# The last attention tile's output product in four pieces with turned tiles between them, and the first MLP product split by token columns

## The reference, cut to what matters

```python
out_a = gqa_axial_attention(qa, ka, va)            # 8 heads of 64: columns 0:512
ob = differential_attention(qb, kb, vb, lam, rel_bias)
out_b = rmsnorm(ob, b_subln_g) * (1.0 - lambda_init)   # 4 heads of 128: columns 512:1024
mixed = jnp.concatenate([out_a, out_b], axis=-1)
x = x + jnp.einsum('bse,ed->bsd', mixed, w_out)

h = rmsnorm(x, mlp_norm_g)
u = jnp.einsum('bsd,df->bsf', h, w_up)             # 1024 -> 4096
u = jnp.square(jax.nn.relu(u))
x = x + jnp.einsum('bsf,fd->bsd', u, w_down)       # 4096 -> 1024
```

## Time and profile before

| | us |
|---|---|
| median of 3 runs | 2272.73 |
| lowest and highest of them | 2269.25, 2276.43 |
| the profiled execution, its own time | 2264.31 |
| its span | 2262.5 |

### The profile page before, as it was taken

How to read it: one execution, slowest core, us unless ns; L and a number is a source line. 1 busy time by engine, 2 the same in 40 slices (tenths; PEclk the granted TensorE clock), 3 DMA queues, 4 the chain that set the end, 5 groups by cost and what they waited for, 6 DMA issues and landing times. The chain is left out here.

```text
span 2262.5 us, 21742 instructions
## 1 busy us (share of the span) xinstructions
PE 2056.5 (91%) x6808; PEld 1127.2 (50%) x6808; DVE 1324.0 (59%) x3030; ACT 880.8 (39%) x2292; POOL 936.7 (41%) x621
## 2 busy tenths in 40 slices
PE   6999998999898989888589999999989998999999
PEld 5787543333333333333233333333345555888887
DVE  6333457777777777787465456465556653433432
ACT  2453314444445444444233345344334332421321
POOL 0692024676555665655246665767711000000000
PEclk9999999999999999999899999999999998999999
DMA  9444249999999999999999999999932002223331
GB/s 379 172 148 147 97 167 397 421 421 416 407 419 408 421 419 404 422 411 421 418 409 407 421 421 400 418 422 422 421 133 84 1 1 93 93 93 103 95 100 56
DMA packets 119219, 650.93 MB, mean 288 GB/s; under 512 B 11048, under 2 KB 29504, under 8 KB 48320
## 3 DMA queue, kind: packets, MB, share of 16 engines
q0 software_dynamic: 73728, 536.90, 57.5%
q1 hardware_dynamic: 42432, 107.32, 13.4%
q10 hardware_dynamic: 2944, 5.33, 0.6%
HBM read 647.41 MB, written 2.10 MB: 287 GB/s over the span
## 5 line engine op out<-in xcount | busy, mean ns | idle before, releaser
L926 PE MATMUL bank<-ring,diag 128*128 128x512 f32 x2048 | 993.1, 612 | 146.8 <-ACT diag L1444 144.9
L600 POOL DMA_INDIRECT ring<-in_uv,idx x512 | 797.8, 1558 | 523.2 <-PE bank L926 255.5
L2058 DVE CUSTOM_DVE_ANT_0 zjunk<-ring,h 128x1024 bf16<-128x1024 f32 x512 | 627.3, 1225 | 420.0 <-DMA ring<-in_uv,idx 418.6
L926 PEld LDWEIGHTS bank<-ring,diag 128*128 128x128 f32 x2048 | 368.6, 191 | 706.4 <-ACT diag L1444 419.5
L1438 ACT ACTIVATE zg<-z 128x1 f32<-128x1 f32 x512 | 103.4, 202 | 689.1 <-DVE z L2058 688.5
L1444 ACT ACTIVATE diag<-ident,weight 128x128 f32<-128x128 f32 x512 | 205.5, 401 | 16.7
L546 POOL TENSOR_SCALAR stats<-stats 128x1 f32<-128x1 f32 (+2 forms) x19 | 4.7, 250 | 331.4 <-ACT slot L1537 119.8
L2231 DVE TENSOR_TENSOR ml_lo<-mlp_raw,ml_hi 128x2048 fp32r<-128x2048 f32 x32 | 73.4, 2293 | 114.4 <-ACT ml_hi L1572 114.4
L856 PE MATMUL bank<-w_q,h2T 128*128 128x512 f32 x256 | 128.6, 593 | 1.8 <-ACT h2T L1334 1.8
L1572 ACT ACTIVATE ml_hi<-mlp_raw 128x2048 fp32r<-128x2048 f32 x32 | 61.1, 1908 | 121.8 <-PE bank L639 107.5
L637 PE MATMUL bank<-hTm_hi,ml_hi 128*128 128x512 f32 x256 | 100.8, 394 | 1.6 <-DVE hTm_lo L2226 1.6
(11 more groups left out here) (242 smaller groups left out, 2619.9 us busy)
## 6 DMA issues: line engine op xcount, KB each, us to landing
ada_w<-in_w_ada SPq DMA_DIRECT2D x24, 1024.0 KB
mlp_raw<-in_w_up SPq DMA_DIRECT2D x16, 1024.0 KB, 5.5
mlp_raw<-in_w_down SPq DMA_DIRECT2D x16, 1024.0 KB, 5.1
win_raw<-in_w_in SPq DMA_DIRECT2D x9, 1024.0 KB, 6.9
w_q<-in_w_query SPq DMA_DIRECT2D x8, 1024.0 KB, 9.3
ring<-in_uv,idx POOLq DMA_INDIRECT x512, 9.8
w_kvb<-in_w_in SPq DMA_DIRECT2D x8, 640.0 KB, 36.3
x<-in_x SPq DMA_DIRECT2D x8, 512.0 KB, 13.0
```

The source lines that it names most:

```text
L600: e.indirect_dma_start(ring[n % RING], None, a["uv"], bass.IndirectOffsetOnAxis(ap=idx[i][:, j:j + 1], axis=0)).then_inc(s[f"d_ring{n % RI ...
L926: t = e.matmul(bank[2 * (i % 2) + half], diag[n % 4], ring[n % RING][:, 1024 + 512 * half:1536 + 512 * half], start=(j == 0), stop=(j == 127))
L2058: e.tensor_tensor_reduce(out=zjunk, in0=ring[n % RING][:, 0:1024], in1=h2[:, i, :], scale=1.0, scalar=0.0, op0=ALU.mult, op1=ALU.add, accu ...
```

## The change

Only the end of attention and the first MLP chunk are touched. Tile 3's output product leaves `output2` and becomes four calls `last_output(half, g)` of four matmuls each: g = 1 takes columns 512:1024 of `mixed` (the differential heads), g = 0 the others, and both add up in the same bank of each output half. Its blocks are turned by `turn_output(g)` into `bank[5]` and `bank[6]`, and ACT copies both halves into `mixT2[1]`; DVE copies none. The turnings of tiles 0, 1 and 2 stand between these pieces. Then both groups of the first chunk are multiplied for the token columns 0:384 (tiles 0 to 2), tile 3 is turned, and the same weights are multiplied once more for columns 384:512.

```diff
             def output2(i):
                 for g in (0, 1):
-                    if i < 3:
-                        q.wait_ge(s["g_sn"], 2 * i + 2)
-                    else:
-                        q.wait_ge(s["v_sn"], 6)
+                    q.wait_ge(s["g_sn"], 2 * i + 2)
...
-            behind = chain(behind, end_norm, output2(3))
-            turned = 0
-            for _ in behind:
-                if turned < 3 and turned in normed:
-                    turn_mlp(turned)
-                    turned += 1
-            for i in range(turned, NT):
-                turn_mlp(i)
+            def turn_output(g):
+                q.wait_ge(s["v_pt2"], 31 if g else 32)
+                if g:
+                    q.wait_ge(s["v_sn"], 6)
+                else:
+                    q.wait_ge(s["v_o2"], 16)
+                turn4(bank[5 if g else 6], o2[3], range(4 * g, 4 * g + 4)).then_inc(s["p_mx2"], 1)
+
+            def last_output(half, g):
+                q.wait_ge(s["v_x2"], 5 + half)
+                q.wait_ge(s["a_mx2"], 4 if g else 5)
+                q.wait_ge(s["d_wo2"], 16)
+                for k in range(4 * g, 4 * g + 4):
+                    t = e.matmul(bank[(4, 7)[half]], mixT2[1][:, k, :], w_out2[:, k, H[half]], start=(k == 4), stop=(k == 3))
+                if g == 0:
+                    t.then_inc(s["p_out2"], 1)
+
+            def up(c, p, cols):
+                wv = [w[c % 2].rearrange("p (k n) -> p k n", k=8) for w in (ml_hi, ml_lo)]
+                for k in range(8):
+                    t = product(bank[4 * (c // 16) + (2 * c + p) % 4][:, cols], [w[:, k, 128 * p:128 * p + 128] for w in wv], [h[:, k, cols] for h in hT3], k == 0, k == 7)
+                return t
+
+            turn_output(1)
+            turn_mlp(0)
+            turn_output(0)
+            last_output(0, 1)
+            turn_mlp(1)
+            last_output(1, 1)
+            last_output(0, 0)
+            turn_mlp(2)
+            last_output(1, 0)
+            q.wait_ge(s["v_t3"], 6)
+            q.wait_ge(s["v_ml"], 1)
+            for p in (0, 1):
+                up(0, p, slice(0, 384))
+            turn_mlp(3)
...
-                        for k in range(8):
-                            t = product(bank[4 * g + f % 4], [w[:, k, 128 * p:128 * p + 128] for w in wv], [h[:, k, :] for h in hT3], k == 0, k == 7)
-                        t.then_inc(s["p_ml"], 1)
+                        up(chunk, p, slice(0 if chunk else 384, 512)).then_inc(s["p_ml"], 1)
```

On ACT:

```diff
+            def turned_output(g):
+                q.wait_ge(s["p_mx2"], 7 if g else 8)
+                q.wait_ge(s["p_out2"], 4)
+                e.activation(mixT2[1][:, 4 * g:4 * g + 4, :], bank[5 if g else 6].rearrange("p (k q) -> p k q", k=4), ACT.Copy).then_inc(s["a_mx2"], 1)
+
+            turned_output(1)
+            turn_mlp(0)
+            for _ in behind:
+                pass
+            turned_output(0)
+            turn_mlp(1)
+            split_chunk(0)
+            turn_mlp(2)
+            square_last(3)
+            turn_mlp(3)
```

On DVE:

```diff
+            next(behind)
+            turn_mlp(0)
+            for _ in behind:
+                pass
+            turn_mlp(1)
+            split_chunk(0)
+            turn_mlp(2)
+            for half in (0, 1):
+                add_output(3, half)
+            norm_last(3)
+            turn_mlp(3)
```

More of the change, by code:

```diff
@@ L1057, in output2 @@
                             yield
[L1058 to L1062, removed]
+                for _ in range(4):
+                    yield
             def last_queries():
@@ L1087, in turn_mlp @@
                     turn4(bank[2 + g], hn3[i], range(4 * g, 4 * g + 4)).then_inc(s["p_t3"], 1)
-            normed = set()
             behind = last_queries()
@@ L1125, in _ @@
                 for c in range(8):
-                    wv = [w[chunk % 2].rearrange("p (k n) -> p k n", k=8) for w in (ml_hi, ml_lo)]
                     q.wait_ge(s["v_t3"], 8)
@@ L1527, in sub_norm2, with square_last @@
                     yield
+            def square_last(i):
+                q.wait_ge(s["v_x2"], 2 * i + 2)
+                q.wait_ge(s["v_hs"], 8)
+                e.activation(hn3[i], x[:, i, :], ACT.Square, accum_out=ss3[:, i:i + 1]).then_inc(s["a_n3"], 1)
             def output2(i):
@@ L1534, in output2 @@
                     yield
-                q.wait_ge(s["v_x2"], 2 * i + 2)
-                q.wait_ge(s["v_hs"], 8)
-                e.activation(hn3[i], x[:, i, :], ACT.Square, accum_out=ss3[:, i:i + 1]).then_inc(s["a_n3"], 1)
+                square_last(i)
                 yield
                 yield
-                normed.add(i)
                 yield
@@ L2192, in sub_norm2, with add_output, norm_last @@
                 yield
+            def add_output(i, half):
+                q.wait_ge(s["p_out2"], 2 * i + half + 1)
+                e.tensor_tensor(x[:, i, H[half]], x[:, i, H[half]], bank[(4, 7)[half]], ALU.add).then_inc(s["v_x2"], 1)
+            def norm_last(i):
+                q.wait_ge(s["g_root"], rooted(f"n{i}"))
+                q.wait_ge(s["d_mg"], 16)
+                e.scalar_tensor_tensor(hn3[i], x[:, i, :], ss3[:, i:i + 1], slot[2], ALU.mult, ALU.mult).then_inc(s["v_n3"], 1)
             def output2(i):
@@ L2202, in output2 @@
                         yield
-                    q.wait_ge(s["p_out2"], 2 * i + half + 1)
-                    e.tensor_tensor(x[:, i, H[half]], x[:, i, H[half]], bank[(4, 7)[half]], ALU.add).then_inc(s["v_x2"], 1)
+                    add_output(i, half)
                 yield
@@ L2207, in output2 @@
                 yield
[L2208 to L2211, removed]
+                norm_last(i)
                 yield
```

## The result

| | median us | lowest to highest | runs |
|---|---|---|---|
| before | 2272.73 | 2264.85 to 2279.16 | 11 |
| the change | 2260.38 | 2252.99 to 2265.98 | 11 |

The ratio is 0.9943 with a 95% interval of 0.992 to 0.9966, so the change is faster by 12.9 us (7.7 to 18.2). The forecast was 2261.1 us, with a range of 2254 to 2269. One execution of a kernel of the experiments (e1) took 5240.42 us, more than twice any other, and is left out of that kernel's median and ratio.

What follows compares the result with a forecast made beforehand. PE bounds the kernel, with waits and clock falls before the first MLP chunk. Roughly 9.0 us of waits and 7 of falls, less 2.7 for splitting, gave 13.3; less 1.7 for a fall, 11.6: 2272.73 to 2261.1 us, range 2254 to 2269.

Steps and rivals of the forecast that it cites:

- Steps 1 to 4: Output product in pieces with tiles 0 to 2 turned between, to 1892.09 us; PE waits 1.26 and 2.67 us covered.
- Steps 5 to 7: First MLP chunk: 384-column matmuls 8.3 us, tile 3's turning and split bare 2.68 us, 128-column matmuls 5.3 us.
- the bounds of 0.067 and 0.22: Price of a 128-column matmul in us: lower from the line through 256 and 512 columns, upper at plain f32 cost.
- the rival at 2266.4: First chunk's 128-column matmuls cost 0.22 us each, 5.3 us more; gain 6.3 us, chance 0.26.
- step 6: Tile 3's turning and split stay bare on PE, 2.68 us; a likely clock fall charged at 1.7 us.
- the case that I gave 0.14: No clock fall behind tile 3's turning: gain 13.3 us, 2259.4 us, chance 0.14.
- the gap in attention: A 1.75 us wait in attention with only short matmuls behind, followed by 3.5 us at clock 0.51.
- Falls inside the output product: Turnings between pieces bring the clock down, 1.7 us per fall; one or two leave 2263 to 2265 us, chance 0.08.
- The slower case: PE at clock 0.50 from the first turnings until the MLP's 512-column matmuls: 2291 us, chance 0.04.
- the one in which the change does nothing: ACT or DVE, around the middle output pieces, arrives over 10 us later than reckoned: 2272.7 us, chance 0.03.
- The range's upper end: Whole kernel at 2269 us: dear 128-column matmuls and a clock fall, with the runs' spread.

Runs made afterwards that it cites:

- e1: Kernel before plus only the first MLP chunk's 384/128 split, output product unbroken: stretch (last `values2` to second relu) 46.90 us, ratio 1.0002.
- e8: The change itself, unaltered, run and traced again: stretch 33.81 us, median 2259.17 us, ratio to before 0.9954.
- e2: The change without the first MLP chunk's split, keeping the output product in pieces with turnings between: stretch 37.81 us, ratio 0.9972.
- e7: Kernel before plus unused f32 matmuls where PE waits, four behind the output product, one behind tile 3's turning: stretch 42.50 us, ratio 0.9982.
- e10: e1 plus one unused 512-column f32 matmul behind tile 3's turning: stretch 43.16 us, ratio to the kernel before 0.998.
- e9: The kernel of e1, unaltered, traced again: stretch 46.94 us, 2278.28 us in one run.

## Why the prediction was right

**What bounds the kernel.** The stretch lost 13.65 us, and e8, whose way up to the stretch was that of before to 0.3 us (1874.9 and 1874.6), has a span 13.3 us shorter. So nothing behind the first chunk takes up time, as I had read from its unbroken 335 us, and the timed 12.9 us (7.7 to 18.2) agrees with it. The times can't tell the forecast's 11.6 us from the 13.3 without a fall; only the traces can. That 2261.1 came within 0.7 us of the median is in part luck: e8's ratio, 0.9954 (0.9933 to 0.9975), gives 10.4 us for the same change.

**Steps 1 to 4, the pieces.** Moved to the start after (14.77 us later), the forecast has tile 1's turning at 1894.63, tile 2's at 1902.49 and tile 3's norm ready at 1911.1. They came at 1894.57, 1902.31 and 1910.92. The waits of 1.26, 2.67 and 0.88 us are gone, and e2 shows the part by itself: 9.6 us, of which about 2.2 hang on the long first fall of the trace before (e7).

**Steps 5 to 7, the split.** 384 columns cost (1914.77 - 1906.80) / 46 = 0.173 us a matmul, as the line through 256 and 512 gave. The short ones, the least sure price, cost (1922.86 - 1917.72) / 46 = 0.112 us for 0.11 reckoned; the bounds of 0.067 and 0.22 are both out, and with the upper the rival at 2266.4. The wait behind the turning is 1.57 us, as before. Chunk 1's split ended at 1918.50 + 2.29 = 1920.8, 2.2 us ahead of its first matmul at 1922.97; I had said 2.0. The split by itself is worth 47.44 - 43.16 = 4.3 us where no fall follows it (e10). With e2's 9.6 that makes 13.9, against 13.65 for both together, so the two parts are nearly independent as long as the clock holds. Without the filled wait they are not: the split alone won 0.5 us (e1), and on top of the pieces 37.81 - 33.79 = 4.0.

**The clock.** This step was wrong for the change: "A fall is likely at step 6. [...] I charge 3.5 us at half pace, 1.7 us." In three traces none came, so the case that I gave 0.14 is the one that happened: 2259.4 on the median, against 2260.38 measured. The gain at full clock was forecast at 13.3 and is 13.65. Such a fall is real: it struck in e1 and e9 at this very place and was absent in e10, where part of the wait was filled. But a turning and a wait of this length don't suffice for it, as I had taken from the gap in attention. There I had its size too small: 10.2 us at half pace in e1 and 13.7 in e9, in place of 3.5. Had it struck in the change, the gain would have been near 8.5 us by e1's length and 6.8 by e9's, an estimate (13.65 less half of the fall).

**The rivals.** Falls inside the output product did not come, in the change or in e2, with sixteen transposes in a row at its start. The Trainium skill's rule (TensorE: Matmul & The Clock Gate, "Part 4: PE-mode transpose") that transposes don't release the clock is neither borne out nor refuted: turning plus waiting preceded each fall in this stretch, turning alone none. My reading that the clock before held until both waits had come was loose: it fell at 1879.5, inside the second of them, which ends at 1880.74. The slower case and the one in which the change does nothing had no sign. The Trainium skill's 81 ns for 128 columns (the same page, "Back-to-back issue gap") does not hold for these fp32r matmuls: 112 ns. The range's upper end, dear matmuls with the spread, should have been 2266.4 + 3.5 = 2269.9; nothing hangs on it.

**What stays open.** Why the change's wait of 1.57 us brings no fall while the same wait in e1 does. The rows ahead of it, 8.3 us of 384-column matmuls at full clock, are the same in both. What differs is what happened earlier (in e1 and e9 a fall of about 10 us that ended some 24 us ahead, in the change none in this stretch) and where in time the wait comes. No experiment separated the two. e10 had the early fall too, 10.2 us, and none behind the turning, so the early fall isn't enough by itself. With two traces of the one kernel and three of the other, chance isn't ruled out either.

## What to carry to other kernels

A tail that every engine walks through one after the other can cost twice on PE: as a wait, and as matmuls at half pace behind it (before, 5.8 us of waits and a fall of 6.9 us), so give PE something to do that doesn't need the tail's result, even if it costs a little. A product cut by token columns is nearly free when each part streams 256 columns: 48 x (0.120 + 0.120 - 0.226) = 0.7 us here, against 48 x (0.173 + 0.112 - 0.226) = 2.8 us for 384 and 128. A part of 128 costs 0.11 us a matmul, as much as a transpose of 128 columns and about what `values2` pays for 64. Compare traces by the stretch that the change touches; here the two profiled spans differed by +1.2 us while the stretch had lost 13.65.

## What the runs showed that I had not expected

- Useless matmuls in PE's waits made the kernel faster (e7: 0.9982, 0.9967 to 0.9998) and a stretch shorter (e10 against e1: 43.16 in place of 46.90 us, one trace against two).
- Identical code ahead of the stretch took 184.3 us in one execution of the change and 196.1 in another, at a mean granted clock of 0.98 and 0.91, with 9.6 us of waiting in both. That is 11.8 of the 14.5 us between these two spans. The 11 runs of each kernel scatter by 13 to 14 us.
- fp32r matmuls at full clock keep a pace of 0.226 us at 512 columns, 0.173 at 384 and 0.120 at 256, and gain almost nothing at 128, with 0.112.
